# Twelve of the eighteen weight units of the second block's input projection are split during the first block's input projection instead of during attention

## What is computed

```python
def reference(x, ...):
    # first block
    h = x
    proj = rms_norm(h, norm_mix_g) @ w_in               # 1024 x 3072: q, k, v of 16 heads of 64
    y_dil = dilated_mixture_attention(...)              # heads 0 to 7, all keys with a distance bias
    y_na = neighbourhood_attention(...)                 # heads 8 to 15, a window on a 16 x 64 grid
    h = h + concat([rms_norm(y_dil), rms_norm(y_na)]) @ w_out
    h = h + hierarchical_moe(rms_norm(h, norm_ffn_g))   # 16 experts, 2 for each token
    x = rms_norm(h, norm_final_g)
    # second block
    h = rmsnorm(x, attn_norm_2)
    q, k, v, g, gk_low, s5_u, rg_x, rg_gate = split(h @ w_in_2)   # 18 tiles of 128 columns in the kernel
    x = x + concat([gla_mixer, s5_mixer, rglru_mixer]) @ w_out_2
    x = x + conv_ffn(rmsnorm(x, mlp_norm_2), ...)
    return rmsnorm(x, final_norm_2)
```

## Time and profile before

| | |
|---|---|
| median of 3 runs | 2444.22 us (2443.25 to 2449.57) |
| the profiled execution's own time | 2445.05 us |
| its span (first to last instruction) | 2443.2 us |
| mean granted TensorE clock | 0.964 of full |
| TensorE matmuls busy | 93% of the span |
| VectorE, ScalarE, GpSimd busy | 48%, 24%, 40% |
| VectorE busy from 40 to 280 us | 189.19 of 240 us |
| TensorE busy from 520 to 655 us | 114.52 of 135 us |
| TensorE busy from 655 to 690 us | 17.34 of 35 us |

### The profile page before, as it was taken

How to read it: one execution, slowest core, us unless ns; L and a number is a source line. 1 busy time by engine, 2 the same in 40 slices (tenths; PEclk the granted TensorE clock), 3 DMA queues, 4 the chain that set the end, 5 groups by cost and what they waited for, 6 DMA issues and landing times.

```text
span 2443.2 us, 28063 instructions
## 1 busy us (share of the span) xinstructions
PE 2263.9 (93%) x10832; PEld 1774.0 (73%) x10832; DVE 1165.3 (48%) x1895; ACT 578.2 (24%) x831; POOL 985.5 (40%) x600
## 2 busy tenths in 40 slices
PE   7999999997699499999599998899999999999997
PEld 5888799987576366665376556678788888888875
DVE  7996644446413222222588777755432233143145
ACT  3101255566533111111231005221210011011011
POOL 2333554468623765700303862233323333333324
PEclk9999999998899699999799999899999999999998
DMA  4231154335622787822722221211111111111103
GB/s 156 78 121 70 42 188 144 120 110 170 201 99 113 271 301 299 324 104 97 280 76 86 103 74 47 104 38 49 43 46 50 52 48 39 61 50 39 58 26 112
DMA packets 89392, 274.33 MB, mean 112 GB/s; under 512 B 6896, under 2 KB 38768, under 8 KB 82096
## 3 DMA queue, kind: packets, MB, share of 16 engines
q1 hardware_dynamic: 71120, 188.84, 22.1%
q0 software_dynamic: 8064, 42.80, 4.8%
q10 hardware_dynamic: 10080, 40.90, 4.3%
HBM read 195.97 MB, written 76.55 MB: 112 GB/s over the span
## 4 chain that ended last, share of the span: by engine, by line
PE 79%; DVE 8%; POOL 5%; DMA 4%; issue 3%; ACT 2%; SPq 0%; DVEq 0%; POOLq 0%; ACTq 0%
PE ps L883 15%; PE ps L885 15%; PE ps L887 15%; PE ps L1005 5%; PE ps L1102 4%; PE ps L982 3%; PE ps L991 3%; PE ps L1086 2%; PE ps L1082 2%; PE ps L1084 2%; PE ps L1083 2%; PE ps L865 1%; PE ps L868 1%; PE ps L867 1%; PE ps L1070 1%
## 5 line engine op out<-in xcount | busy, mean ns | idle before, releaser
L883 PE MATMUL ps<-work_part 128*128 128x512 f32 x1760 | 547.9, 393 | 2.6 <-DVE work L2385 1.7
L887 PE MATMUL ps<-work_part 128*128 128x512 f32 x1760 | 542.4, 389 | 0.0
L661 POOL CAST work_part<-ring 128x1024 fp32r<-128x1024 f32 (+2 forms) x124 | 118.5, 956 | 786.1 <-PE ps L887 659.6
L883 PEld LDWEIGHTS ps<-work_part 128*128 128x128 f32 x1760 | 329.8, 188 | 76.9 <-issue 6.5
L887 PEld LDWEIGHTS ps<-work_part 128*128 128x128 f32 x1760 | 330.6, 188 | 69.2
L885 PE MATMUL ps<-work_part 128*128 128x512 f32 x1152 | 354.6, 389 | 0.0
L665 POOL TENSOR_TENSOR work_part<-ring,work_part 128x1024 fp32r<-128x1024 f32 (+2 forms) x124 | 281.2, 2268 | 15.9 <-PE ps L1300 6.1
L885 PEld LDWEIGHTS ps<-work_part 128*128 128x128 f32 x1152 | 216.2, 188 | 44.9
L885 PE MATMUL ps<-hT_part,work_part 128*128 128x512 f32 x608 | 188.0, 390 | 0.0
L1005 PE MATMUL ps<-work,hT 128*128 128x64 f32 x1376 | 174.3, 276 | 2.6 <-ACT hT L1433 2.1
L2033 DVE TENSOR_TENSOR hT<-ps,hT 128x1024 f32<-128x1024 f32 x40 | 49.0, 1225 | 261.5 <-PE ps L887 245.0
(11 more groups left out here) (376 smaller groups left out, 3490.2 us busy)
## 6 DMA issues: line engine op xcount, KB each, us to landing
pages<-w_moe SPq DMA_DIRECT2D x16, 2048.0 KB, 9.7
ring<-w_up_units SPq DMA_DIRECT2D x44, 512.0 KB, 3.2
ring<-w_in_units SPq DMA_DIRECT2D x42, 512.0 KB, 3.7
w_parts<-work_part SPq DMA_DIRECT2D x36, 512.0 KB, 3.6
work_part<-w_parts SPq DMA_DIRECT2D x36, 512.0 KB, 4.1
pages<-w_moe SPq DMA_DIRECT2D x16, 1024.0 KB, 7.0
x_slots<-hT SPq DMA_DIRECT2D x31, 512.0 KB, 5.2
work<-x_slots ACTq DMA_DIRECT2D x31, 512.0 KB, 5.7
```

The source lines that it names most:

```text
L661: pool.tensor_copy(WHI[n % 2][:, 0:cols], w).then_inc(whi_ready, 1)
L883: pe.matmul(ps[:, c], whi[:, w], hi[k][:, c], start=(k == 0), stop=False)
L887: mm = pe.matmul(ps[:, c], wlo[:, w], hi[k][:, c], start=False, stop=(k == len(hi) - 1))
```

## The change

`EARLY = 12`: the units 0 to 11 of the second block's input projection are split right after `split(1)` to `split(12)`, in the first projection. Raw units come into pages 12 and 14 of the work area in turn; the high part goes to page 13 or 15 and the low part over the raw unit. SP parks unit n after the ring load of unit n+5, waits for the two stores, and then loads raw unit n+2. Units 12 to 17 are split after heads 1 to 6, through ring page 0 as before. The zeros of `x_slots` are no longer tied to the parked units: the first four go out at once when the zero tile is set, the rest as scores are done. ScalarE waits for the parked units before it writes pages 12 and 14. A scratch page of the first norm moves from 15 to 11, and six semaphores are merged into three.

```diff
+EARLY = 12
@@
+        parts_order = [0]
+        for u in range(1, U_OUT):
+            parts_order += [u] + ([U_IN2 + u - 1] if u <= EARLY else [])
+        parts_order += list(range(U_IN2 + EARLY, U_OUT2)) + list(range(U_OUT, U_IN2)) + list(range(U_OUT2, len(units)))
@@
+        EARLY_RAW = [Wp[12], Wp[14]]
+        def in2_split(n):
+            if n < EARLY:
+                return Wr[13 + 2 * (n % 2)][:, :], Wr[12 + 2 * (n % 2)][:, :]
+            return Wr[38][:, :], Wr[37][:, :]
@@
             def load_in2(n):
-                sp.dma_start(ring[:, 0, :], units[U_IN2 + n]).then_inc(w_loaded[0], 16)
+                if n < EARLY:
+                    sp.dma_start(EARLY_RAW[n % 2], units[U_IN2 + n]).then_inc(early_loaded[n % 2], 16)
+                else:
+                    sp.dma_start(ring[:, 0, :], units[U_IN2 + n]).then_inc(w_loaded[0], 16)
 
             def park_in2(n):
+                hi, lo = in2_split(n)
                 sp.wait_ge(wlo_ready, order_of[U_IN2 + n] + 1)
-                sp.dma_start(w2_parts[n, 0], Wr[38][:, :].bitcast(f32)).then_inc(parked, 16)
-                sp.dma_start(w2_parts[n, 1], Wr[37][:, :].bitcast(f32)).then_inc(parked, 16)
-                sp.wait_ge(parked, 32 * (n + 1))
-                if n + 1 < 18:
-                    load_in2(n + 1)
+                sent = early_parked[n % 2] if n < EARLY else parked
+                sp.dma_start(w2_parts[n, 0], hi.bitcast(f32)).then_inc(sent, 16)
+                sp.dma_start(w2_parts[n, 1], lo.bitcast(f32)).then_inc(sent, 16)
@@
-                    load_in2(0)
+                    load_in2(EARLY)
                     sp.wait_ge(zero_set, 1)
-                    for n in range(U_OUT2 - U_IN2):
-                        park_in2(n)
-                        for b in range(2 * n, min(2 * n + 2, NBLK)):
+                    for b in range(NBLK):
...
+                        n = EARLY + (b - 5) // 2
+                        if b % 2 == 1 and EARLY <= n < 18:
+                            park_in2(n)
+                            if n + 1 < 18:
+                                sp.wait_ge(parked, 32 * (n + 1 - EARLY))
+                                load_in2(n + 1)
@@
+                if u == 4:
+                    load_in2(0)
+                    load_in2(1)
+                if 5 <= u < EARLY + 5:
+                    n = u - 5
+                    park_in2(n)
+                    sp.wait_ge(early_parked[n % 2], 32 * (n // 2 + 1))
+                    if n + 2 < EARLY:
+                        load_in2(n + 2)
@@
             for n in range(24):
                 split(n)
+                if 1 <= n <= EARLY:
+                    split_in2(n - 1)
@@
                 pool.wait_ge(qk_parts, 6 * h + 6)
-                split_in2(h)
-            split_in2(16)
-            split_in2(17)
+                if 1 <= h <= 18 - EARLY:
+                    split_in2(EARLY + h - 1)
```

More of the change, by code:

```diff
@@ L149, in build @@
         x_loaded = [sem(f"x_loaded{i}") for i in range(4)]
+        early_loaded = [sem(f"early_loaded{i}") for i in range(2)]
+        early_parked = [sem(f"early_parked{i}") for i in range(2)]
         cst_loaded = sem("cst_loaded")
         strip_loaded = [sem(f"strip_loaded{i}") for i in range(2)]
-        x_again = sem("x_again")
         s5_loaded = sem("s5_loaded")
@@ L221, in build @@
         U_UP = U_OUT2 + 8
-        PARKED = 32 * (U_OUT2 - U_IN2)
+        PARKED = 32 * (U_OUT2 - U_IN2 - EARLY)
         split_units = list(range(0, U_IN2)) + list(range(U_OUT2, len(units)))
         split_of = {u: n for n, u in enumerate(split_units)}
-        parts_order = list(range(0, U_OUT)) + list(range(U_IN2, U_OUT2)) + list(range(U_OUT, U_IN2)) + list(range(U_OUT2, len(units)))
+        parts_order = [0]
+        for u in range(1, U_OUT):
+            parts_order += [u] + ([U_IN2 + u - 1] if u <= EARLY else [])
+        parts_order += list(range(U_IN2 + EARLY, U_OUT2)) + list(range(U_OUT, U_IN2)) + list(range(U_OUT2, len(units)))
         order_of = {u: n for n, u in enumerate(parts_order)}
@@ L242, in build @@
         for u in parts_order:
+            if U_IN2 <= u < U_IN2 + EARLY:
+                continue
             at_ring = 0 if in2(u) else ring_at(u)
@@ L315, in build @@
         U_QKV += [take(1) for m in range(2, 7)]
-        n_mix = add_late_norm(Hp, "norm_mix", [Wp[22], Wp[23], Wp[15]], mix_use, take(1), (BHI, [hTr[t][:, :] for t in range(NT)]))
+        n_mix = add_late_norm(Hp, "norm_mix", [Wp[22], Wp[23], Wp[11]], mix_use, take(1), (BHI, [hTr[t][:, :] for t in range(NT)]))
         U_QKV += [take(1) for m in range(7, 16)]
@@ L455, in build @@
         emptied[P_LOGIT] = (logit_ready, 1)
-        emptied[P_ROUTE], emptied[P_RANK] = (gdiff_ready, 1), (rank_read, 1)
+        emptied[P_ROUTE], emptied[P_RANK] = (route_diff, 1), (rank_read, 1)
         for b in range(NBLK):
@@ L669, in split_in2 @@
                 u = U_IN2 + n
[L670 to L674, removed]
+                hi, lo = in2_split(n)
+                if n < EARLY:
+                    raw = EARLY_RAW[n % 2]
+                    pool.wait_ge(early_loaded[n % 2], 16 * (n // 2 + 1))
+                    if n >= 2:
+                        pool.wait_ge(early_parked[n % 2], 32 * (n // 2))
+                else:
+                    raw = ring[:, 0, :]
+                    pool.wait_ge(w_loaded[0], raw_loads[u])
+                    if n > EARLY:
+                        pool.wait_ge(parked, 32 * (n - EARLY))
+                pool.tensor_copy(hi, raw).then_inc(whi_ready, 1)
                 pool.wait_ge(whi_ready, order_of[u] + 1)
-                pool.tensor_tensor(lo, ring[:, 0, :], hi.bitcast(f32), ALU.subtract).then_inc(wlo_ready, 1)
+                pool.tensor_tensor(lo, raw, hi.bitcast(f32), ALU.subtract).then_inc(wlo_ready, 1)
                 pool.wait_ge(wlo_ready, order_of[u] + 1)
@@ L1162, in _ @@
                 if c == 0:
-                    pe.wait_ge(cst_again, 16)
+                    pe.wait_ge(reloaded, 32)
                 for gate in range(2):
@@ L1500, in _ @@
                                scale=std[:, n_ffn["index"] % 4, tt:tt + 1]).then_inc(xtm_ready, 1)
[L1502 to L1505, removed]
+            act.wait_ge(route_diff, 1)
+            act.activation(R("gd"), R("gd"), ACT.Exp).then_inc(route_exp, 1)
+            act.wait_ge(route_diff, 2)
+            act.activation(R("d1"), R("d1"), ACT.Exp).then_inc(route_exp, 1)
             act.wait_ge(x_scattered, 16 * 2 * NT)
```

29 lines of the change are left out of this document (15 added, 14 removed).

## The result

The changed kernel takes 2464.41 us (median of 4 runs, 2460.88 to 2470.21); the kernel before takes 2445.59 us beside it (2443.25 to 2449.57). The ratio is 1.0078, with a 95% interval from 1.0053 to 1.0102: slower by about 19 us. The predicted time was 2460, which is 4.4 us under the median. The profiled execution took 2460.88 us, with a span of 2459.1 and a mean granted clock of 0.962.

A forecast was written before the change was run, and what follows sets the result against it. It took VectorE, standing still while GpSimd splits, to bound the first projection, and unit 24's late split the end of attention. 2445.05 + 29.6 + 1 - 1 - 15 = 2459.7, said as 2460; range 2454 to 2470.

The forecast's parts named there:

- Twelve splits more: First projection: each split holds VectorE 2.9 us, the eighth turn ends 39 later; less 9.4 slack, third v unit 29.6 later.
- The sign that the prediction named: First projection: a VectorE turn with two ordinary and two new splits takes 22.8 us; under 19 would prove the prediction wrong.
- The first stop isn't added: TensorE stands about 17 us for VectorE's inverse norms after unit 6, not summed because the eighth turn is the later gate.
- TensorE's stop before the v units: First projection: TensorE stands some 5 us before the first v transposition or the third v unit.
- GpSimd's own time: First projection: an extra pair takes GpSimd 3.5 us, covered by 7.3 us idle before a split, so costs nothing.
- Transfers: First projection: twelve loads and 24 stores of 512 KB in SP's queue cost nothing.
- The strip behind four zero stores: Attention's start: head 0's strip lands later beside four stores of zeros, costing 1 us, bounds 0 and 3.
- Inside attention: VectorE's 1.36 us wait for head 15's strip, issued after a split, shrinks; 1 us gained.
- The end of attention: Unit 24's split no longer waits for second-block units; the output projection starts sooner, gaining 15 us, bounds 13 and 16.
- No slowdown, or one that the slack takes: Rival: the splits don't slow VectorE further, or its slack takes them; 2430 us, chance 0.06.
- Half the loss: Rival: back-to-back pairs let VectorE through, 1.7 us lost per split; 2444 us, no change; chance 0.10.
- The end not shortened: Rival: unit 24 still waits, for the last zeros or another load; 2476 us, chance 0.08.

The follow-up runs named there:

- e1: Changed kernel with the twelve early units' loads and stores kept, but their cast and subtraction on GpSimd each replaced by a one-column copy; 2437.34 us.
- e2: Changed kernel with the subtraction of each early pair replaced by a shorter one-input copy of the high part; 2451.16 us.
- e3: Changed kernel with six second-block units split early instead of twelve, after ordinary splits 1 to 6; 2451.46 us.
- e5: Changed kernel with six early units, their pairs placed after ordinary splits 7 to 12, loads and stores moved along; 2448.57 us.
- e7: Changed kernel with the stores of zeros held until head 0's strip has landed; 2463.64 us.
- e8: The changed kernel run once more, unaltered, on the same chip; 2469.11 us, ratio 1.0093 to the kernel before.
- e4: Changed kernel with two early units, sixteen split one per head after its strip is issued, and zero stores following parked units again; 2433.04 us.
- e6: Changed kernel with two early units split after ordinary splits 3 and 4, zero stores following parked units; 2434.39 us.

## Why the prediction was right, and where its sizes were off

*Twelve splits more* (forecast + 29.6). The mechanism is shown: e1 takes GpSimd's work away and the delay goes with it, e2 shortens the work and the delay shrinks in proportion. The price of 2.9 us per pair measured 2.8 over the whole projection, but not everywhere: VectorE's inverse norms are made 28.55 us later (114.08 against 85.53) with ten splits more ahead of them, 2.9 for each, and in the turns a split costs less. The sign that the prediction named, 22.8 us for a turn with two ordinary and two new splits, is met by 22.9 only by luck, since that turn holds four and a half: (22.90 - 14.10) / (15.47 - 3.43) is 0.73 us for each us of GpSimd, or 2.5 for a split. The eighth turn came 36.7 us late instead of 39, mostly because one ordinary split more fell into the stretch and not one and a half. Less the slack of 9.4 that is 27.3, and the third v unit came 27.4 late.

*The first stop isn't added* (forecast 17 us, not in the sum). It was 17.2 us. For twelve pairs the step holds, since the later gate decided. But the prediction thought of this stop as idle time alone. It also takes the clock down, to 0.82 in the 12.6 us after it:

```profile
115.36:128.00 12.64, 12.64 (x42) 8.96 (x43) 11.71 (x51) 1.02 (x1) 0.00 (x0) 0.82 0.07 31
```

With six pairs (e3) just this gate decided, which the expectation for e3, made from the prediction's slack, missed by some 8 us. A sum made only with the last gate is right only when that gate is the later one.

*TensorE's stop before the v units* (forecast some 5 us): 2.67 + 0.66 + 0.63 = 4.0 us. Only 1.3 of them are at the two places that the prediction named; the first is a tile earlier, and the granted clock was 0.80 in the 8.6 us behind it (231.4 to 240.0).

*GpSimd's own time* (nothing): it holds. GpSimd still stands idle for 3.89 us before the split at 98.36.

*Transfers* (nothing): shown by e1.

*The strip behind four zero stores* (+ 1, bounds 0 and 3): 2.4 us. This term was mis-sized; the time was nearer to the upper bound, and the reason given for the lower end (large packets) didn't hold.

*Inside attention* (- 1): the stretch gave + 1.8 instead, from 30.0 us of delay at the first exponential to 31.8 at the end. The term itself came, with 0.7: no wait for a strip is left in the last heads, and the delay falls from 32.5 at head 14's first row on VectorE (654.58 against 622.12) to 31.8 at head 15's (667.58 against 635.78). What goes the other way lies ahead of that, where it rises from 29.6 (619.56 against 589.92, head 12) to 32.5. There the windows of the changed kernel show

```profile
630.00:640.00 10.00, 9.59 (x43) 9.40 (x44) 6.04 (x20) 5.93 (x16) 4.30 (x5) 0.50 0.33 99
640.00:650.00 10.00, 10.00 (x48) 9.52 (x47) 3.90 (x17) 4.36 (x13) 7.14 (x5) 0.55 0.27 65
```

Some 20 us at half the clock. The kernel before has such a stretch too, from 590 to about 605 us, a little shorter.

The experiments show one more thing here that the prediction didn't think of. SP's loads of the output projection's first two units, which went out behind the last head before, can go out beside the strip of head 14. That strip lands 6.0 to 7.5 us after its issue in the changed kernel, e1, e2, e3, e5, e7 and e8, where it took 3.4 before. The changed kernel and e8 (6.1 and 6.0) have no wait from it; the other five wait 2.7 to 3.1 us, as in e1 and e3 (waits from 560 to 740 us):

```profile
DVE hT L2035 <- DMA hT<-na_strip: 3.1, 1, 3.1
```

```profile
DVE hT L2024 <- DMA hT<-na_strip: 2.7, 1, 2.7
```

In e4 and e6, where those loads leave after the last zeros, the strip took 4.9 and 3.5 us and nothing waits. That the loads are the cause is argued from these rows; no run changes them alone.

*The end of attention* (- 15, bounds 13 and 16): 12.8 in the changed kernel, just under the lower bound; 13.0 in e4 (12.5 at the restart, with the end of attention 0.5 later), and 12.8 to 13.9 in the others, taken in the same way. The steps were as forecast: unit 24's split starts with the last scores, the scaled rows are late next (4.57 us, "some 5"). The size is off by the clock. The sixteen transpositions took 3.65 us instead of 1.9 and the 24 matmuls behind them 6.4 instead of 5.6, so that 700.99 less the shift of 31.8 is 669.2, where 666.6 was forecast. The granted clock was 0.71 from 690.96 to 700.99. The prediction named this ("up to 2 us of the gain go") and took 15, near the other bound; it was 2.6.

*The sum.* 27.4 + 2.4 + 0.2 to the first exponential, 1.8 inside attention and - 12.8 at its end make 19.0 at the restart, and 2445.05 + 19.0 is 2464, near the measured median. In the profiled execution 3.1 us came back later, between the end of the experts and the first units of the second block's projection (from 1127 to 1435 us of the kernel before), without a wait that could be named, and gave 2460.9. That the forecast's 2459.7 is so close to this one execution is luck: 2.2 too much for the splits stand against 1.4 too little for the strip, 2.8 for the heads and 2.2 for the end, together 4.2 too little, and of these the 3.1 took most back. Against the median, 2464.41, the 4.2 remain.

*The rivals.* No slowdown, or one that the slack takes: false for twelve pairs, and true for two, which is e4 and e6; their eighth turns, 8.8 and 7.8 us late, stay inside the slack of 9.4 us at the v units that the prediction read from the trace. Half the loss: false, 2.8 us and not 1.7. The end not shortened: false, the wait for unit 24's split is gone.

## What to carry to other kernels

Work moved off a busy stretch onto an engine that stands idle can still be paid for by a third engine: before moving it, look at how long the neighbour's smallest instructions last beside it, and count the moved work against the neighbour's slack at every gate, the first one too. Then move only as much as the end needs. Here two of the eighteen units gave the whole gain of the end (13.0 us, against 12.8 with twelve) inside a slack of 9.4 us, 2433 to 2434 us instead of 2445 to 2447; with twelve the end is no shorter and the v units are 27 us late. A stop of TensorE costs more than its idle time, 3.2 us more behind 11.3 here, where no later gate takes it in.

## What the runs showed of the hardware that was not expected

**GpSimd is held by VectorE too.** Beside the parts of x, where VectorE works on two inputs of 1024 columns without a gap, GpSimd's timeline shows

```profile
23.52 3.33 POOL L711 CAST work_part<-work 128x1024 fp32r<-128x1024 f32 x1 [9.12 <-DMA work<-w_in_units]
...
26.93 3.26 POOL L713 TENSOR_TENSOR work_part<-work,work_part 128x1024 fp32r<-128x1024 f32 x1
```

and VectorE's

```profile
23.54 1.27 DVE L1820 SCALAR_TENSOR_TENSOR hT_part<-hT,cst,work_part 128x1024 fp32r<-128x1024 f32 x1
24.74 1.21 DVE L1779 TENSOR_TENSOR work<-work 128x1024 f32<-128x1024 f32 x1
25.87 2.05 DVE L1820 SCALAR_TENSOR_TENSOR hT_part<-hT,cst,work_part 128x1024 fp32r<-128x1024 f32 x1
...
27.85 3.42 DVE L1779 TENSOR_TENSOR work<-work 128x1024 f32<-128x1024 f32 x1
```

A cast that takes 1.04 us elsewhere takes 3.33, while two VectorE instructions run beside it at full speed; then the subtraction has its turn, and VectorE's instruction takes 3.42 instead of 1.21. Neither engine is always the loser.

The row at 146.60 of e2, a GpSimd copy with one input, has a VectorE instruction beside it that is stretched all the same, to 1.25 us, where the same instruction on as many columns takes 0.48 at 112.60. So it isn't the number of GpSimd's inputs that decides. The Trainium skill says in "GPSIMD Engine Reference", section "Key points", that GpSimd contends with VectorE instructions in a two-port mode or with two SBUF inputs. The inputs meant are VectorE's: the stretched instruction is a `scalar_tensor_tensor` that reads two tensors in SBUF, and the trace agrees. Whether the stretched TENSOR_SCALAR rows, with one tensor each, run in a two-port mode no row here tells.

**TensorE's clock falls in the last heads of attention in every profile, at different places.** In windows of 10 us from 590 to 650 us the lowest granted clock is 0.50 (its level of 1.2 GHz) at 590 before, at 630 in the changed kernel and at 600 in e6, 0.52 at 640 in e5, and between 0.54 and 0.68 in the six others, e4's 0.68 being the highest. The delay changed inside attention between a gain of 1.5 us (e4, 2.0 late at the start and 0.5 at the end) and a loss of 5.7 (e5, 12.4 and 18.1, of which the wait for head 14's strip is a part). What picks the place stays open; it was not tried.
